# The expert stage of a decoder block: six experts written out, against hardware loops on four engines

## The chip, the core and the metric

The kernel runs on one core of a Trainium2 chip. A core has five engines with an instruction stream each: PE (TensorE, matrix products), DVE (VectorE), ACT (ScalarE), POOL (GpSimd) and SP (SyncE, which here only issues DMA transfers). Each stream is read by a sequencer of its own, and the streams wait for one another by semaphores. The time is the device time of one execution in microseconds (us); lower is better.

## What is computed

Two layers of a decoder on 256 tokens of 1024 channels, all in float32. Each layer has a mixer (a gated MLP over positions beside multi-head latent attention) and a channel part with SwiGLU: dense in the first layer, in the second eight experts of which each token takes two. The change is in the experts:

```python
logits = (xt @ w_router + b_router).astype(jnp.float32)
top_val, top_idx = lax.top_k(logits, TOP_K)          # 2 of 8
gates = jax.nn.softmax(top_val, axis=-1)
...
def run_block(args):                                  # one expert on up to 128 tokens
    tok, e = args
    xb = x_pad[tok]
    hb = jax.nn.silu(xb @ w1[e]) * (xb @ w3[e])       # 1024 -> 3584
    return hb @ w2[e]                                 # 3584 -> 1024
...
out = jnp.zeros((N + 1, D), h.dtype).at[buf_tok].add(yb)[:N]   # yb weighted by the gates
```

## The kernel before

Weights come from HBM in chunks of 128 x 2048 floats (1 MB). SP loads each into one of seven slots of `raw`. For full float32 accuracy a chunk is split in two parts that PE reads faster: ACT copies `raw` to `hi` (rounded, L511), DVE computes `lo = raw - hi` (L883), both into one of three slots, and PE makes three products per piece, `hi*hi`, `lo*hi` and `hi*lo` (`three`, L1358 to L1360; each matmul has its own weight load, which the profile calls PEld). One chunk is twelve such matmuls of 512 columns. At the end of a chunk PE raises the semaphore `used`, which frees the `hi`/`lo` slot for ACT; DVE raises `raw_done`, for which PE waits before it starts a chunk and SP before it loads into the `raw` slot again.

An expert is an item of 42 chunks (`PER_ITEM`), in seven groups `g`: two chunks of `w1`, two of `w3`, and two of `w2` of the group before. `w2` of the last group is done in the next item, so each item is entangled with its neighbour. `item(i, par, first, ahead)` writes out one item on an engine; `par` says which half of the token tiles it uses. Besides the chunks, an item holds work for the next one: `select` (DVE, at `g == 2`) copies the next expert's positions and gates and writes the matrices that pick its tokens (`one_hot`; and `gate_hot`, the same with the gate weights, into `r4[:, 256:512]`), `slot_rows` and `rows` find the rows to gather, `turn_rows`, `gathered` and `gathered_lo` bring the next tokens in (the last two groups).

Items 0 and 7 have other arguments than the six between. All eight are written out: on SP by `for i in range(1, EXPERTS)` (L342), on ACT, DVE and PE by `for i in range(1, EXPERTS - 1)` (L778, L1340, L1762). So item numbers are constants, and so are the values of all waits. POOL's eight steps are written out too. Behind them stands a hardware loop over up to three spare items for experts with more than 128 tokens (`If(spare > 0)`, L347, L784, L1345, L1767). With these inputs there is no spare item (the 336 loads of expert weights are 8 x 42), and each engine jumps over it. In this loop the same functions are called with `i` in a register, so the code for that exists. Each engine's order is the order of the code; there is no scheduler. `Fori` repeats a body on the one engine that calls it, with no barrier between engines.

Of the kernel before, what the change touches and what calls it, by code (L numbers as in the profile page):

```python
# [25 lines left out]
T = SEQ // P  # L26
# [15 lines left out]
EXPERTS = 8  # L42
# [133 lines left out]
def build(nc, A, out):  # L176
    with ExitStack() as ctx:
# [32 lines left out]
        ms, rstd = sb("mean_sq", [P, 4]), sb("rstd", [P, 4])  # L210
# [103 lines left out]
        @block.sync  # L314
        def _(sp):
            sp.dma_start(cols[:, :], A["cols"]).then_inc(consts_in, 16)
            sp.dma_start(cbc[:, :], A["c"].to_broadcast([P, D])).then_inc(cbc_in, 16)
            for r, (kind, n, q) in enumerate(STREAM):
                if r >= NRAW:
                    sp.wait_ge(raw_done, r - NRAW + 1)  # L320
                if kind == "ada":
                    l, v = ADA[n]
                    src, e = A["w_ada"][l, v, q], CH
                else:
                    _, t, (a, b), e = WEIGHTS[n]
                    src = A[t][a, b]
                sp.dma_start(raw[:, r % NRAW, 0:e], src).then_inc(raw_full[r % NRAW], 16)
                if r == 1:
                    sp.dma_start(x[:, :, :], A["x"].rearrange("b (t p) d -> p (b t) d", p=P)).then_inc(x_in, 16)

            def item_loads(i, chunks, expert):
                for c, kind, g, half, before_ in chunks:
                    sp.wait_ge(raw_done, i * PER_ITEM + (NR + c - NRAW + 1))
                    e = expert - 1 if before_ else expert
                    src = A["moe_" + kind]
                    src = src[e, g, half] if isinstance(e, int) else \
                        src[bass.ds(e, 1), g, half, :, :].rearrange("e p n -> p (e n)")
                    slot = (NR + c) % NRAW
                    sp.dma_start(raw[:, slot, :], src).then_inc(raw_full[slot], 16)

            item_loads(0, item_order(True), 0)
            for i in range(1, EXPERTS):  # L342
                item_loads(i, item_order(False), i)
            item_loads(EXPERTS - 1, LAST, EXPERTS - 1)
            sp.wait_ge(route_ready, 1)
            spare = sp.value_load(info[0:1, ITEMS:ITEMS + 1], min_val=0, max_val=SPARE)
            with sp.If(spare > 0):  # L347
                with sp.Fori(EXPERTS, ITEMS) as i:
                    with sp.If(i < spare + EXPERTS):
                        expert = sp.value_load(info[0:1, bass.ds(i, 1)], min_val=0, max_val=EXPERTS - 1)  # L350
                        item_loads(i, item_order(True) + LAST, expert)
            for t in range(T):
                sp.wait_ge(x_done, 2 * L * T - T + 1 + t)
                sp.dma_start(out[0, t * P:(t + 1) * P, :], x[:, t, :]).then_inc(out_done, 16)
            sp.wait_ge(out_done, 16 * T)
# [130 lines left out]
        def _(act):  # L486
# [252 lines left out]
            def item(i, par, first, ahead):  # L739
                if first:  # L740
                    for h in range(2):
                        gather_hi(i, par, h)
                    if not ahead:
                        item_hi(i, 0, 2)
                at = [(3 if ahead else 2) if first else 0]

                def upto_c(c):
                    item_hi(i, at[0], c + 1)
                    at[0] = max(at[0], c + 1)

                for g in range(NG):
                    c = spot("w1", g, 1, first)
                    if g == 1 and not first:
                        upto_c(c + 1)
                        weighted_y(i - 1, 1 - par, spot("w2", NG - 1))
                    upto_c(min(c + 2, PER_ITEM - 1))
                    act.wait_ge(used, i * PER_ITEM + (NW + c + 1))
                    act.activation(hs[g], ps[:, g % 2, :], ACT.Silu).then_inc(m_silu, 1)
                    if g:
                        hidden_hi(i, g - 1)  # L760
                    elif not first:
                        hidden_hi(i - 1, NG - 1)
                    if g == 3 and not ahead:
                        act.wait_ge(m_gt, i - (EXPERTS - 2))
                        act.activation(r4[:, 512:512 + SEQ], ps[:, 7, 0:SEQ], ACT.Copy).then_inc(m_gtc, 1)
                    if ahead and g >= NG - 2:
                        upto_c(min(c + 3, PER_ITEM - 1))
                        gather_hi(i + 1, 1 - par, g - (NG - 2))
                upto_c(PER_ITEM - 1)
# [5 lines left out]
                copy_y(i, PER_ITEM - 1)  # L775

            item(0, 0, True, True)
            for i in range(1, EXPERTS - 1):  # L778
                item(i, i % 2, False, True)
            item(EXPERTS - 1, 1, False, False)  # L780
            drain(EXPERTS - 1)
            act.wait_ge(route_ready, 1)
# [14 lines left out]
        def _(dve):  # L797
# [346 lines left out]
            for t in range(T):  # L1144
                dve.wait_ge(router_full, t + 1)
                m = dve.tensor_tensor(lg[:, t, :], ps[:, R_BANK[t], 0:E], rb[:, :], ALU.add)
            link(m)

            for t in range(T):
# [3 lines left out]
                m = dve.tensor_tensor(eq[:, t], other, own, ALU.is_equal)  # L1153
            link(m)
            for t in range(T):
                m = dve.tensor_tensor(eq[:, t], eq[:, t], lt_mask[:, :, :], ALU.mult)
# [51 lines left out]
            def one_hot(t, value):  # L1208
                return dve.tensor_scalar(r4[:, t * P:(t + 1) * P], slots[:, :], pg[:, t:t + 1], value, ALU.is_equal, ALU.mult)

            def gate_hot(t):
                return dve.tensor_scalar(r4[:, 256 + t * P:256 + (t + 1) * P], slots[:, :], pg[:, t:t + 1], vals[:, t, 2:3],
                                         ALU.is_equal, ALU.mult)

            def select(i, by_row):

                dve.tensor_copy(pg[:, :], pos_tab[:, :, bass.ds(i, 1)].rearrange("p t o -> p (t o)"))
                dve.tensor_copy(vals[:, :, 2], gate_tab[:, :, bass.ds(i, 1)].rearrange("p t o -> p (t o)")).then_inc(v_loop, 1)
                dve.wait_ge(v_loop, i + 1)
                for t in range(T):  # L1220
                    m = one_hot(t, 1.0 if by_row else rstd[:, T + t:T + t + 1])
                    if not by_row or i == EXPERTS - 1:
                        m = gate_hot(t)
                m.then_inc(m_pos, 1)

            def select_first():
# [110 lines left out]
                dve.memset(small[:, 0:1], 0.0)  # L1337

            item(0, 0, True, True)
            for i in range(1, EXPERTS - 1):  # L1340
                item(i, i % 2, False, True)
            item(EXPERTS - 1, 1, False, False)
            drain(EXPERTS - 1)
            spare = dve.value_load(info[0:1, ITEMS:ITEMS + 1], min_val=0, max_val=SPARE)
# [10 lines left out]
        def _(pe):  # L1355
# [403 lines left out]
                    scatter(i, q, DRAIN[q])  # L1759

            item(0, 0, True, True)
            for i in range(1, EXPERTS - 1):  # L1762
                item(i, i % 2, False, True)
            item(EXPERTS - 1, 1, False, False)
            drain(EXPERTS - 1)
            spare = pe.value_load(info[0:1, ITEMS:ITEMS + 1], min_val=0, max_val=SPARE)
# [78 lines left out]
```

## Time and profile before

| | us |
|---|---|
| median of 3 runs | 1586.76 |
| lowest and highest | 1585.12, 1586.84 |
| the profiled execution | 1586.84 |
| its span, first to last instruction | 1585.1 |
| TensorE clock granted, mean | 0.986 |

The page of the profile gives the busy time of each engine, the chain of work that ended last (92% of it PE, 5% DVE) and the costliest groups of instructions. The expert stage begins near 607 us and ends near 1568 us. Instructions of a sequencer alone (branches, waits, register operations; marked with a q behind the engine, as PEldq) are not counted as busy. A granted clock of 1.00 is 2.4 GHz and 0.50 is 1.2 GHz.

### The profile page before, as it was taken

The page shows a single profiled execution, that of the slowest core. Times are in us where ns is not written, and L with a number is a line of the kernel's source. Part 1 is how long each engine was busy: PE and PEld are TensorE (multiplying, and loading weights), DVE is VectorE, ACT ScalarE, POOL GpSimd, SP SyncE. Part 2 cuts the span into 40 slices and gives each one's busy share as a digit, 9 for nine tenths or more (in the row PEclk, how much of TensorE's full clock was granted, in tenths as well). Part 3 has the DMA queues.
Part 4 walks back from the last instruction along what each step waited for, and adds up shares of the span by engine and source line. Part 5 has one row for each costly group of instructions (what it writes and reads, how often), then busy time and mean ns, then how long its engine had stood idle before and what let it go on. Part 6 is the DMA issues. An engine that isn't in the chain of part 4 may idle for free.

```text
span 1585.1 us, 19800 instructions
## 1 busy us (share of the span) xinstructions
PE 1515.7 (96%) x8112; PEld 1310.0 (83%) x8112; DVE 1333.5 (84%) x1298; ACT 1011.8 (64%) x869; POOL 73.8 (5%) x103
## 2 busy tenths in 40 slices
PE   2999989999899988999999999999999999999996
PEld 2899979999789977888888888888888888888884
DVE  6688977775888768999999999999999998998885
ACT  3673444444466445777777777777777777777773
POOL 6000000000000000000000000000000000000000
PEclk9999999999999998999999999999999999999998
DMA  9757957986755855999999999999999999999990
GB/s 374 284 195 276 343 224 292 299 265 208 234 209 212 258 208 204 364 382 359 390 381 358 397 383 354 401 379 356 401 372 363 397 379 362 388 377 367 409 382 29
DMA packets 72977, 507.98 MB, mean 320 GB/s; under 512 B 8240, under 2 KB 8368, under 8 KB 14128
## 3 DMA queue, kind: packets, MB, share of 16 engines
q1 hardware_dynamic: 68672, 491.94, 81.9%
q0 software_dynamic: 4208, 14.70, 3.3%
q8 instruction: 66, 1.08, 0.3%
q14 instruction: 31, 0.25, 0.0%
HBM read 499.78 MB, written 6.83 MB: 320 GB/s over the span
## 4 chain that ended last, share of the span: by engine, by line
PE 92%; DVE 5%; ACT 1%; DMA 1%; issue 1%; SPq 0%; DVEq 0%; ACTq 0%
PE ps L1358 29%; PE ps L1360 28%; PE ps L1359 28%; PE ps L1728 2%; DVE raw L816 1%; PE ps L1375 1%; DMA x_tok<-in_x_dram 1%; PE ps L1496 1%; PE ps L1479 1%; DVE r L902 1%; DVE x_tok L940 1%; ACT r L523 0%; DVE lo L855 0%; PE ps L1425 0%; DVE hT_lo L908 0%
## 5 line engine op out<-in xcount | busy, mean ns | idle before, releaser
L883 DVE TENSOR_TENSOR lo<-raw,hi 128x2048 fp32r<-128x2048 f32 x336 | 766.3, 2290 | 94.5 <-ACT hi L511 93.7
L511 ACT ACTIVATE hi<-raw 128x2048 fp32r<-128x2048 f32 x336 | 644.6, 1919 | 198.3 <-PE ps L1360 198.3
L1358 PE MATMUL ps<-hi,hT_hi 128*128 128x512 f32 (+2 forms) x1088 | 427.6, 393 | 12.2 <-DVE hT_lo L908 8.8
L1360 PE MATMUL ps<-hi,hT_lo 128*128 128x512 f32 (+2 forms) x1088 | 421.0, 387 | 0.0
L1359 PE MATMUL ps<-lo,hT_hi 128*128 128x512 f32 (+2 forms) x1088 | 420.5, 386 | 0.0
L1358 PEld LDWEIGHTS ps<-hi,hT_hi 128*128 128x128 f32 x1088 | 205.3, 189 | 58.0 <-issue 13.1
L855 DVE TENSOR_TENSOR lo<-raw,hi 128x2048 fp32r<-128x2048 f32 (+2 forms) x87 | 189.9, 2187 | 62.7 <-ACT hi L495 61.3
L1360 PEld LDWEIGHTS ps<-hi,hT_lo 128*128 128x128 f32 x1088 | 205.2, 189 | 41.0
L1359 PEld LDWEIGHTS ps<-lo,hT_hi 128*128 128x128 f32 x1088 | 205.5, 189 | 37.6
L1358 PE MATMUL ps<-hi,bT_hi 128*128 128x512 f32 (+1 forms) x576 | 224.6, 390 | 1.8 <-DVE bT_lo L1272 1.8
L1359 PE MATMUL ps<-lo,bT_hi 128*128 128x512 f32 (+1 forms) x576 | 223.7, 388 | 0.0
L1360 PE MATMUL ps<-hi,bT_lo 128*128 128x512 f32 (+1 forms) x576 | 223.5, 388 | 0.0
L495 ACT ACTIVATE hi<-raw 128x2048 fp32r<-128x2048 f32 (+2 forms) x87 | 158.4, 1824 | 93.1 <-PE ps L1360 89.7
L1358 PE MATMUL ps<-hT_hi,hi 128*128 128x256 f32 x608 | 173.0, 285 | 1.7 <-DVE hT_lo L908 1.7
L1360 PE MATMUL ps<-hT_hi,lo 128*128 128x256 f32 x608 | 172.1, 283 | 0.0
L1359 PE MATMUL ps<-hT_lo,hi 128*128 128x256 f32 x608 | 172.0, 283 | 0.0
L1358 PEld LDWEIGHTS ps<-hi,bT_hi 128*128 128x128 f32 x576 | 108.6, 188 | 26.0 <-issue 2.8
L1360 PEld LDWEIGHTS ps<-hi,bT_lo 128*128 128x128 f32 x576 | 108.5, 188 | 21.8
L1359 PEld LDWEIGHTS ps<-lo,bT_hi 128*128 128x128 f32 x576 | 108.4, 188 | 20.9
L816 DVE SCALAR_TENSOR_TENSOR raw<-raw,c_rows 128x1024 f32<-128x1024 f32 x96 | 113.6, 1221 | 9.9 <-DMA raw<-in_w_ada_dram 9.8
L1358 PEld LDWEIGHTS ps<-hT_hi,hi 128*128 128x128 f32 x608 | 116.7, 192 | 2.6 <-DVE hT_lo L908 1.4
L1359 PEld LDWEIGHTS ps<-hT_lo,hi 128*128 128x128 f32 x608 | 116.6, 192 | 0.3
(255 smaller groups left out, 1177.9 us busy)
## 6 DMA issues: line engine op xcount, KB each, us to landing
raw<-in_moe_w_dram SPq DMA_DIRECT2D x336, 1024.0 KB, 7.1
raw<-in_w_ada_dram SPq DMA_DIRECT2D x48, 1024.0 KB, 6.1
raw<-in_w_fg_dram SPq DMA_DIRECT2D x11, 1024.0 KB, 7.4
raw<-in_w_fu_dram SPq DMA_DIRECT2D x11, 1024.0 KB, 6.7
raw<-in_w_fd_dram SPq DMA_DIRECT2D x11, 1024.0 KB, 6.9
raw<-in_w_ga_dram SPq DMA_DIRECT2D x8, 1024.0 KB, 5.9
raw<-in_w_gb_dram SPq DMA_DIRECT2D x8, 1024.0 KB, 5.2
raw<-in_w_ab_dram SPq DMA_DIRECT2D x8, 1024.0 KB, 4.9
```

The lines of the kernel that those rows point to most:

```text
L495: act.activation(hi[:, s % NSPLIT, 0:e], raw[:, r % NRAW, 0:e], ACT.Copy).then_inc(hi_done, 1)
L511: act.activation(hi[:, s, :], raw[:, slot, :], ACT.Copy).then_inc(hi_done, 1)
L816: m = dve.scalar_tensor_tensor(w, w, 1.0, cbc[:, :], ALU.mult, ALU.mult, accum_out=av[:, k:k + 1])
L855: dve.tensor_tensor(lo[:, s % NSPLIT, 0:e], raw[:, r % NRAW, 0:e], hi[:, s % NSPLIT, 0:e].bitcast(f32), ALU.subtract).then_inc(raw_done, 1)
L883: dve.tensor_tensor(lo[:, s, :], raw[:, slot, :], hi[:, s, :].bitcast(f32), ALU.subtract).then_inc(raw_done, 1)
L902: m = dve.tensor_scalar(hf[:, k, :], ps[:, X_BANKS[n][b], (k % 2) * SEQ:(k % 2 + 1) * SEQ], AB[:, n, 0, k:k + 1], AB[:, n, 1, k:k + 1], AL ...
L940: dve.scalar_tensor_tensor(x[:, t, :], y_sb[:, t, :], rstd[:, t:t + 1], x[:, t, :], ALU.mult, ALU.add).then_inc(x_done, 1)
L1358: pe.matmul(o, wh, mh, start=first, stop=False)
L1359: pe.matmul(o, wh, ml, start=False, stop=False)
L1360: return pe.matmul(o, wl, mh, start=False, stop=last)
L1375: m = pe.matmul(ps[:, X_BANKS[n][k // 2], (k % 2) * SEQ + t * P:(k % 2) * SEQ + (t + 1) * P], x[:, t, k * P:(k + 1) * P], diag[:, t, :], s ...
L1728: m = pe.transpose(ps[:, 6, c * P:(c + 1) * P], hs[g][:, c * P:(c + 1) * P], ident[:, :])
```

## The change

SP's seven items become one hardware loop of seven passes. On ACT, DVE and PE the six items become a loop of three passes with two items in the body, one for each value of `par`. `i` is then a register (or computed from one), and so are the values of the waits in the body. On DVE `select` no longer depends on whether `i` is the last item: it writes `gate_hot` every time. In the changed kernel the lines of DVE and PE have numbers one higher, since ACT's part is a line longer.

```diff
             item_loads(0, item_order(True), 0)
-            for i in range(1, EXPERTS):
+            with sp.Fori(1, EXPERTS) as i:
                 item_loads(i, item_order(False), i)
             item_loads(EXPERTS - 1, LAST, EXPERTS - 1)
...
             item(0, 0, True, True)
-            for i in range(1, EXPERTS - 1):
-                item(i, i % 2, False, True)
+            with act.Fori(0, EXPERTS // 2 - 1) as j:
+                item(j * 2 + 1, 1, False, True)
+                item(j * 2 + 2, 0, False, True)
             item(EXPERTS - 1, 1, False, False)
...
                 for t in range(T):
-                    m = one_hot(t, 1.0 if by_row else rstd[:, T + t:T + t + 1])
-                    if not by_row or i == EXPERTS - 1:
-                        m = gate_hot(t)
+                    one_hot(t, 1.0 if by_row else rstd[:, T + t:T + t + 1])
+                    m = gate_hot(t)
                 m.then_inc(m_pos, 1)
```

The six lines of ACT stand in the same words for DVE and PE.

What moves in the streams. PE, from the last matmuls of an even item to the next item, before:

```order
L1358 MATMUL ps<-hi,bT_hi 128x512
L1359 MATMUL ps<-lo,bT_hi 128x512
L1360 MATMUL ps<-hi,bT_lo 128x512
L1358 MATMUL ps<-hi,hT_hi 128x512 [waits raw_done,m_x,m_silu]
L1359 MATMUL ps<-lo,hT_hi 128x512
L1360 MATMUL ps<-hi,hT_lo 128x512
```

and in the changed kernel the end of the loop's body:

```order
L1359 MATMUL ps<-hi,bT_hi 128x512
L1360 MATMUL ps<-lo,bT_hi 128x512
L1361 MATMUL ps<-hi,bT_lo 128x512
L1763 REGISTER_ALU
L1763 COMPARE_AND_BRANCH
```

and the head of the body, to which the branch goes back:

```order
L1763 ISA
L1672 ISA [waits m_silu]
L1666 ISA [waits m_x]
L1359 MATMUL ps<-hi,hT_hi 128x512 [waits raw_done]
L1360 MATMUL ps<-lo,hT_hi 128x512
```

Two rows are added at the loop's end and three at its head, and two of the three waits now stand on register instructions (ISA and REGISTER_ALU). The body is 1197 rows on PE (1084 of them matmuls), 265 on DVE, 240 on ACT and 102 on SP.

DVE at `select`, in an item between the first and the last, before:

```order
L1272 TENSOR_TENSOR bT_lo<-ps,bT_hi 128x4x128 [waits m_hh]
L883 TENSOR_TENSOR lo<-raw,hi 128x2048 [waits hi_done] x2
L1268 TENSOR_TENSOR r<-r,ps 128x512 [waits used,m_silu]
L883 TENSOR_TENSOR lo<-raw,hi 128x2048 [waits hi_done] x4
L1272 TENSOR_TENSOR bT_lo<-ps,bT_hi 128x4x128 [waits m_hh]
L1217 COPY pg<-pos_tab 128x2
L1218 COPY slot_vals<-gate_tab 128x2
L1209 TENSOR_SCALAR r<-slots,pg 128x128 [waits v_loop]
L1209 TENSOR_SCALAR r<-slots,pg 128x128
L883 TENSOR_TENSOR lo<-raw,hi 128x2048 [waits hi_done] x2
```

and in the changed kernel:

```order
L1272 TENSOR_TENSOR bT_lo<-ps,bT_hi 128x4x128 [waits m_hh]
L1218 ISA
L1218 COPY pg<-pos_tab 128x2
L1219 REGISTER_ALU
L1219 COPY slot_vals<-gate_tab 128x2
L1220 REGISTER_ALU
L1210 TENSOR_SCALAR r<-slots,pg 128x128 [waits v_loop]
L1213 TENSOR_SCALAR r<-slots,pg,slot_vals 128x128
L1210 TENSOR_SCALAR r<-slots,pg 128x128
L1213 TENSOR_SCALAR r<-slots,pg,slot_vals 128x128
L883 REGISTER_ALU
L884 TENSOR_TENSOR lo<-raw,hi 128x2048 [waits hi_done]
```

Two `gate_hot` (L1213) and register instructions ahead of each wait are added. ACT, the head of its loop in the changed kernel, from the branch into it:

```order
L778 UNCONDITIONAL_BRANCH
L778 ISA
L510 ISA [waits raw_full2]
L511 ACTIVATE hi<-raw 128x2048 [waits used]
L510 REGISTER_ALU [waits raw_full3]
L511 ACTIVATE hi<-raw 128x2048 [waits used]
L757 REGISTER_ALU
L758 ACTIVATE r<-ps 128x512 [waits used]
```

The same stretch was only the ACTIVATE rows before; each of the others carries the register value, or the first of two waits, of the one behind it.

## Rows read from the trace of the kernel before

**Rows 1.** busy time by engine, page part 1: busy us (share) xinstructions

```profile
PE 1515.7 (96%) x8112; PEld 1310.0 (83%) x8112; DVE 1333.5 (84%) x1298; ACT 1011.8 (64%) x869; POOL 73.8 (5%) x103
```

**Rows 2.** busy by stretch, experts 1 to 6: us busy (x) per engine, PEclk, DMA

```profile
722.87:1442.74 719.87, 719.39 (x3275) 592.98 (x3276) 653.20 (x448) 538.01 (x355) 28.91 (x12) 1.00 0.99 378
```

**Rows 3.** waits in that stretch: who waited for whom, us, times, longest

```profile
PEld ps L1358 <- issue: 3.5, 8, 0.5
PEld ps L1358 <- DVE lo L883: 2.4, 6, 0.4
```

**Rows 4.** timeline, weight loads at chunk starts: start us, us, what, [idle before]

```profile
961.94 0.19 PEld L1358 LDWEIGHTS ps<-hi,hT_hi 128*128 128x128 f32 x1 [0.47 <-issue]
...
1006.82 0.19 PEld L1358 LDWEIGHTS ps<-hi,bT_hi 128*128 128x128 f32 x1
...
1009.54 0.19 PEld L1358 LDWEIGHTS ps<-hi,bT_hi 128*128 128x128 f32 x1
...
1197.83 0.19 PEld L1358 LDWEIGHTS ps<-hi,bT_hi 128*128 128x128 f32 x1
...
1200.97 0.19 PEld L1358 LDWEIGHTS ps<-hi,hT_hi 128*128 128x128 f32 x1 [0.47 <-issue]
...
1206.90 0.19 PEld L1358 LDWEIGHTS ps<-hi,hT_hi 128*128 128x128 f32 x1
...
1320.50 0.19 PEld L1358 LDWEIGHTS ps<-hi,hT_hi 128*128 128x128 f32 x1 [0.47 <-issue]
...
1440.10 0.19 PEld L1358 LDWEIGHTS ps<-hi,hT_hi 128*128 128x128 f32 x1 [0.47 <-issue]
```

**Rows 5.** timeline of DVE and ACT around the start of expert 5

```profile
1195.16 2.29 DVE L883 TENSOR_TENSOR lo<-raw,hi 128x2048 fp32r<-128x2048 f32 x1 [0.31 <-ACT hi L511]
...
1198.57 6.70 DVE L883 TENSOR_TENSOR lo<-raw,hi 128x2048 fp32r<-128x2048 f32 x3
...
1198.31 1.92 ACT L511 ACTIVATE hi<-raw 128x2048 fp32r<-128x2048 f32 x1 [0.80 <-PE ps L1360]
1201.03 1.92 ACT L511 ACTIVATE hi<-raw 128x2048 fp32r<-128x2048 f32 x1 [0.80 <-PE ps L1360]
```

**Rows 6.** single lines of the sequencers: duration ns min/median/max, first and last start

```profile
L1767 PEldq COMPARE_BRANCH  x1: 3854/3854/3854, 1569.9 to 1569.9; - x1
...
L1766 PEldq FUSED_REGOPS  x1: 165/165/165, 1569.6 to 1569.6; - x1
...
L1345 DVEq COMPARE_BRANCH  x1: 76/76/76, 1574.4 to 1574.4; - x1
...
L784 ACTq COMPARE_BRANCH  x1: 45/45/45, 1568.7 to 1568.7; - x1
```

**Rows 7.** the program's end: PE's timeline, stretch 1569 to 1575, its DMA queue

```profile
1569.04 3.70 PE L1749 MATMUL ps<-r 128*128 128x512 f32 x8 [1.17 <-ACT r L730]
...
1569.00:1575.00 6.00, 3.70 (x8) 1.44 (x8) 2.81 (x5) 1.49 (x2) 0.00 (x0) 1.00 0.04 8
...
q8 instruction: 2, 0.03, 2.7%
```

**Rows 8.** PE's semaphore instruction ahead of a chunk, expert 5

```profile
L1665 PEldq EVENT_SEMAPHORE  x1: 51/51/51, 1200.9 to 1200.9; - x1
```

**Rows 9.** DMA issues, page part 6: xcount, KB each, us to landing

```profile
raw<-in_moe_w_dram SPq DMA_DIRECT2D x336, 1024.0 KB, 7.1
```

**Rows 10.** timeline of DVE behind `select`, experts 3 and 6

```profile
1004.26 4.57 DVE L883 TENSOR_TENSOR lo<-raw,hi 128x2048 fp32r<-128x2048 f32 x2
...
1363.17 4.48 DVE L883 TENSOR_TENSOR lo<-raw,hi 128x2048 fp32r<-128x2048 f32 x2
```

**Rows 11.** busy by stretch where PE stood idle, columns as in rows 2

```profile
612.70:617.60 4.90, 3.34 (x15) 2.77 (x16) 4.69 (x11) 3.14 (x4) 0.00 (x0) 1.00 0.59 221
...
1558.70:1560.60 1.90, 0.07 (x1) 0.08 (x1) 1.77 (x2) 0.60 (x1) 0.00 (x0) 1.00 0.00 0
...
1560.80:1564.10 3.30, 3.30 (x9) 2.52 (x9) 0.00 (x0) 0.00 (x0) 0.00 (x0) 0.50 0.00 0
```

More of the change, by code:

```diff
@@ L1339, in _ @@
             item(0, 0, True, True)
-            for i in range(1, EXPERTS - 1):
-                item(i, i % 2, False, True)
+            with dve.Fori(0, EXPERTS // 2 - 1) as j:
+                item(j * 2 + 1, 1, False, True)
+                item(j * 2 + 2, 0, False, True)
             item(EXPERTS - 1, 1, False, False)
@@ L1761, in _ @@
             item(0, 0, True, True)
-            for i in range(1, EXPERTS - 1):
-                item(i, i % 2, False, True)
+            with pe.Fori(0, EXPERTS // 2 - 1) as j:
+                item(j * 2 + 1, 1, False, True)
+                item(j * 2 + 2, 0, False, True)
             item(EXPERTS - 1, 1, False, False)
```

## Prediction

> **What bounds the kernel now.** I read the busy table first: TensorE (PE) is busy 96% of the span, VectorE (DVE) 84%, ScalarE (ACT) 64% [rows 1]. The table by stretch comes second. From 722.87 to 1442.74 us, six experts long, PE is busy 719.39 of 719.87 us at the full granted clock, DVE 653, and the DMA share is 0.99 [rows 2]. So whatever is added there hurts only if it delays PE. The waits of that stretch come third: in 720 us PE's weight loads wait 2.4 us for the `lo` copy and 3.5 us for "issue" [rows 3]. Work goes round in a ring: PE frees a slot, ACT makes `hi` (1.92 us), DVE makes `lo` (2.29 us) [rows 5], PE uses the pair three chunks later.
>
> The timeline says how tight the ring is. At the start of the sixth expert (i = 5) the last chunk of the one before starts on PE at 1197.83, and its `lo` ended at 1195.16 + 2.29 = 1197.45, 0.38 us sooner. The next chunk starts at 1200.97, 3.14 us later instead of the 2.72 us between the chunk starts at 1006.82 and 1009.54, because DVE comes late there: three `lo` back to back from 1198.57 [rows 4, 5]. An expert takes 1320.50 - 1200.97 = 119.53 us.
>
> **The loops.** Experts 1 to 6 become a loop of three passes over two experts on PE, DVE and ACT; SP's loop has seven passes of one. Each of the first three engines therefore takes a backward branch twice, SP six times. Three things are new: the branch, register instructions ahead of waits, and `gate_hot` in every `select`.
>
> *The branch.* The trace of before holds one taken branch per engine, the jump over the spare experts. On DVE and ACT it took 76 and 45 ns, on PE 3854 ns, and around PE's the queue q8 read two blocks of instructions [rows 6, 7]. PE's jump skips 609 rows of the order with 554 matmuls, the other two 138 and 121. The new backward jump of PE crosses 1197 rows, further still, so I charge it as a fetch: 3.854 us. I read the Trainium skill, "Runtime: NRT & Kernel Launch", section "Instruction fetch mechanics", the same way: a taken branch whose target lies outside the two pages held must wait for the page. The trace agrees for PE. Another rule speaks for a much lower price and is rival C.
>
> What of 3.854 us does PE feel? Matmuls are handed over in advance: at 1569.04 eight matmuls of L1749 start which last 3.70 us, and the branch behind them began at 1569.9, beneath them [rows 6, 7]. So the branch starts when the last chunk has been handed over, at about 1197.5 (its `lo` end), plus one register instruction, taken as the 51 ns of PE's semaphore instruction [rows 8]: 1197.55. It ends at 1201.40. Three "ISA" rows stand at the head of the body; as a fused register operation costs 165 ns [rows 6], 0.50 us, plus 0.07 us from semaphore to weight load: 1201.97. Without a branch that load came at 1200.97. Loss: 1.0 us per branch when the DMA queues are idle as they were at 1569 to 1575 (DMA share 0.04) [rows 7]. In the expert stage the share is 0.99 [rows 2], and a 1 MB load lands after 7.1 us [rows 9] while one is wanted every 2.72: about 2.6 are under way at a time, and behind one of them the fetch would be 2.7 us later. I take 0.6, nearer to no delay because instructions have a queue of their own. So 1.6 us per branch, bounds 1.0 and 3.7, and 3.2 us for two.
>
> *DVE's and ACT's branches* cross 265 and 240 rows, about twice what they jumped cheaply, so they may cost 0.05 to 3.9 us. ACT's pass ends with the `hi` of 1198.31, DVE's with the second of the three `lo` from 1198.57; the `hi` of 1201.03 and the third `lo` (about 1203.0) are the first work of the next pass [rows 5]. At 3.9 us ACT's branch would end at 1198.4 + 3.9 = 1202.3, two fused operations of 165 ns [rows 6] bring its `hi` to 1202.6, it is done at 1204.6, and `lo` at 1206.9; DVE's own branch (from 1200.3) ends sooner than that. PE needs this chunk at 1206.90 [rows 4] plus its own 1.6 us = 1208.5. Hidden, by 1.6 us. If PE's branch were free the margin would be zero, and these branches would cost 0 to 0.5 us. SP's loads run seven slots ahead: the slot ring is 7 x 2.72 = 19 us, of which landing takes 7.1 and `hi` and `lo` 4.3; 7 us are left against 3.9. Nothing.
>
> *Register instructions.* One stands before nearly every wait. On PE it runs while the sequencer would wait anyway (a chunk is handed over within a chunk's 2.72 us). On DVE and ACT it runs below a working instruction of 0.6 to 2.3 us. Exposed is only the chain of `rows()`, four short instructions that follow one another by semaphores with `lo` behind them. Of its register rows one is a fused operation (165 ns on PE, rows 6), most of it beside a copy; I charge 0.06 us per expert, bounds 0 and 0.3. Over six: 0.4 us. SP has one load to issue per 2.72 us and several us of lead: nothing.
>
> *gate_hot.* Before, only `select(7)` did it, so the trace has both forms. In expert 3 the `lo` behind it starts at 1004.26, 42.32 us after PE's start at 961.94; in expert 6, with `gate_hot`, at 1363.17, 42.67 us after 1320.50 [rows 4, 10]. So `lo` is 0.35 us later, and a margin takes most of it: expert 6 lasts 1440.10 - 1320.50 = 119.60 us, 0.07 more than expert 5 [rows 4]. Six times: 0.4 us, bounds 0.4 and 1.4.
>
> **Sum.** 3.2 + 0.4 + 0.4 = 4.0 us on the profiled execution's own 1586.84 us (span 1585.1 and 1.7 around it), which is 0.08 above the median of 1586.76: 1590.8 us. About 0.2%, 3.2 us, is what a measurement of this kernel tells from no change, so the forecast is just on the slower side.
>
> **Rivals.**
>
> A, the forecast: 1.0 to 2.0 us per back edge, 1589.6 to 1592. Chance 0.42.
>
> B, each back edge costs more. The fetch takes the whole 2.7 us more, and PE's idle time brings the half clock. The trace shows it once near the end: from 1558.7 to 1560.6 PE was busy 0.07 of 1.90 us, and from 1560.8 to 1564.1 the granted clock was 0.50, with 9 matmuls in 3.30 us [rows 11]; that is 1.2 instead of 2.4 GHz and costs half the stretch, 1.6 us. Per edge 1.0 + 2.7 + 1.6 = 5.3, twice 10.6, plus 0.8: 1598.2. For it: total idle at the edge would be 0.4 + 3.7 us. Against: the stretch from 612.7 holds 1.5 us in which PE was idle and stays at 1.00 [rows 11], and at the forecast's 1.6 us the idle time, 2.0 us, lies near either example. Chance 0.24.
>
> C, the back edge is nearly free, as DVE's and ACT's in the trace: then only 0.8 us is added: 1587.6, no measurable change. The 3854 ns would be something else of that one place (it is PE's last instruction, with matmuls still running). The Trainium skill, "Advanced Engine Details and Errata", section "Control Flow Timing", gives about 108 ns for a compare-and-branch; by that the two edges would cost 0.2 us. The trace has 45 and 76 ns and the one 3854. Chance 0.19.
>
> D, faster. At present an instruction with two waits is preceded by a separate semaphore instruction, 51 ns on PE [rows 8]; in the loop the first wait rides on the register instruction instead, ahead of the last one. Where DVE is late, PE's gap would shrink, at the expert's start above all (3.14 - 2.72 = 0.42 us). In six experts PE's loads wait 3.5 + 2.4 = 5.9 us [rows 3]; all of it gone, with the 0.8 us still to pay, gives 1581.7. It decides only if the edge is free and more than 0.5 us per expert comes back, while what it can remove directly is under 0.1 us at each place. Chance 0.08.
>
> E, the register instructions are not hidden: PE, DVE and ACT each pay at every chunk. With 252 chunks in the loop and 0.05 us each, 12.6 us more: 1600 or above. Against it: the margin of 0.38 us and more before each chunk. Chance 0.07.
>
> Slower by over 0.2% is above 1589.9: three quarters of A, B and E, 0.63. Same: the rest of A and C, 0.29. Faster 0.08. The range leaves out D, most of E and the far end of B: 1587.2 to 1598.5.
>
> **What would show it.** PE's compare-and-branch twice with about 4 us, and an idle PE of 1 to 2 us beyond the present 0.4 at the starts of experts 3 and 5, nothing such at 2, 4 and 6. DVE and ACT branches long or short, without PE waiting for `lo` behind them. Expert 4 or 6 lasting about 119.6 to 119.7 us (119.53 before) checks the small terms; 120 or more would be E. Branches of 0.1 us on PE would refute the largest step; granted clock 0.5 in the expert stage would be B.

## The result

The changed kernel takes 1602.63 us (median of 4 runs, 1599.17 to 1603.6) against 1586.75 us in the same comparison; the ratio is 1.0099, with a 95% interval of 1.0082 to 1.0116. The forecast was 1590.8 us, with a range of 1587.2 to 1598.5. The direction was right, the size was not: +15.9 us instead of +4.0.

The page of the changed kernel, parts 1 and 3 (columns as in rows 1; a queue's packets, MB, share):

```profile
PE 1519.5 (95%) x8112; PEld 1312.9 (82%) x8112; DVE 1334.7 (83%) x1310; ACT 1012.0 (63%) x869; POOL 73.7 (5%) x103
...
q8 instruction: 71, 1.16, 0.3%
q14 instruction: 25, 0.20, 0.0%
```

PE has the same 8112 matmuls, busy 3.8 us longer, in a span that is 15.6 us longer (1600.7 against 1585.1): most of the loss is idle time. q8, which brings PE's instructions, made 71 reads of 16 KB; before it made 66. One such read is called a block below; it holds 256 instructions, which the counts of the experiments bear out. (The 1197 rows of PE's loop are, with one weight load for each matmul and the sequencer's own, 2290 instructions in the trace, nearly nine blocks.) The waits of PE's weight loads over the six experts, beside [rows 3]:

```profile
PEld ps L1361 <- issue: 8.7, 2, 5.0
PEld ps L1359 <- DVE lo L884: 6.5, 11, 3.1
PEld ps L1359 <- issue: 2.1, 2, 1.7
```

The line to notice is the first. L1361 is the third matmul of a group of three; no semaphore is waited for there, and [rows 3] has no such entry. Now it waits twice, 8.7 us in all, for nothing that a semaphore shows. Busy time by stretch shows where (columns as in rows 2):

```profile
720.00:955.00 235.00, 235.00 (x1073) 193.93 (x1072) 213.75 (x152) 175.63 (x118) 9.70 (x4) 1.00 0.99 379
955.00:975.00 20.00, 13.99 (x53) 10.79 (x52) 11.45 (x7) 8.76 (x5) 0.00 (x0) 0.83 0.82 320
975.00:1195.00 220.00, 220.00 (x1003) 181.58 (x1002) 199.29 (x139) 164.37 (x109) 9.61 (x4) 1.00 0.96 370
1195.00:1222.00 27.00, 21.18 (x90) 16.87 (x89) 17.86 (x15) 14.92 (x10) 0.00 (x0) 0.87 0.88 330
1222.00:1450.00 228.00, 228.00 (x1043) 188.36 (x1042) 206.98 (x147) 171.10 (x114) 9.62 (x4) 1.00 0.97 372
```

Outside the two short stretches PE is busy without a break. Both short ones hold a back edge of PE's loop. The timeline of the weight loads at the first (the counterpart of 961.94 in rows 4):

```profile
961.87 0.19 PEld L1361 LDWEIGHTS ps<-hi,bT_lo 128*128 128x128 f32 x1
965.14 0.19 PEld L1359 LDWEIGHTS ps<-hi,hT_hi 128*128 128x128 f32 x1 [3.08 <-DVE lo L884]
965.25 0.19 PEld L1360 LDWEIGHTS ps<-lo,hT_hi 128*128 128x128 f32 x1
969.22 0.29 PEld L1361 LDWEIGHTS ps<-hi,hT_lo 128*128 128x128 f32 x1 [3.79 <-issue]
969.39 0.34 PEld L1359 LDWEIGHTS ps<-hi,hT_hi 128*128 128x128 f32 x1
969.82 0.33 PEld L1360 LDWEIGHTS ps<-lo,hT_hi 128*128 128x128 f32 x1
```

There are three losses, one behind the other. PE stands until 965.14, for its branch; that the row names DVE's `lo` only means that this semaphore came last by the profile, for the sequencer was inside the branch from 959.2 for 5.6 us (below). It then does two matmuls and stands again until 969.22. From there the loads are 0.43 us apart instead of 0.227: half the clock, 1.2 instead of 2.4 GHz. The same happens at 1210.74 and 1216.00. The branch lines, q8 in the stretches 958 to 970 and 1204 to 1217, and the clock after each second gap:

```profile
L1763 PEldq COMPARE_BRANCH  x3: 83/4191/5626, 959.2 to 1452.4; - x3
...
q8 instruction: 2, 0.03, 1.1%
...
q8 instruction: 2, 0.03, 0.9%
...
969.10:972.60 3.50, 3.38 (x8) 2.70 (x9) 0.00 (x0) 0.00 (x0) 0.00 (x0) 0.50 0.97 396
1215.90:1219.40 3.50, 3.40 (x9) 2.73 (x10) 0.00 (x0) 0.00 (x0) 0.00 (x0) 0.57 0.89 346
```

Two blocks are read at each edge where the argument had one. When they are read shows in shorter stretches, 962 to 963 and 966.5 to 967.5:

```profile
q8 instruction: 1, 0.02, 6.7%
...
q8 instruction: 1, 0.02, 6.0%
```

The first read starts at 962.33, while the branch runs (959.15 to 964.78). The second starts at 966.99, 2.2 us after the branch has ended, and PE goes on 2.2 us behind that. The branch lines of the other engines' loops (ACT, DVE, SP):

```profile
L778 ACTq COMPARE_BRANCH  x3: 40/45/45, 959.9 to 1453.1; - x3
...
L1340 DVEq COMPARE_BRANCH  x3: 50/56/76, 961.8 to 1455.0; - x3
...
L342 SPq COMPARE_BRANCH  x7: 40/45/50, 820.1 to 1551.4; - x7
```

All are short. q14 brings the other engines' instructions, 8 KB at a time: its 31 reads become 25 with their loops and stay 31 where PE alone has one (the first experiment). Between 930 and 1560 us, while these three engines go round their loops, it reads nothing at all.

The account in the profiled executions goes by the start of each expert on PE (its first weight load): 723.77, 843.08, 965.14, 1089.94, 1210.74, 1336.27 and 1455.67 us in the changed kernel, so experts 1 to 6 last 119.31, 122.06, 124.80, 120.80, 125.53 and 119.40 us. Against the mean of the two undisturbed ones, 119.355, the first stalls cost 2.7 and 1.4 us (they fall into experts 2 and 4), the second stalls with the half clock 5.4 and 6.2 (experts 3 and 5). Unrounded that is 15.8 us. Beside it 0.9 us were lost ahead of expert 1 (723.77 against 722.87), and 1.1 us was won over the six experts, which took 119.50 to 119.60 each before.

### The profile page after: what moved, and what is told of

The parts are those of the page before. It is cut to its first block, busy times and chain, and to the rows that moved or that the text cites. A ratio compares the mean times of both kernels' runs of the same rounds, so it can differ in the third digit from the quotient of the medians.

```text
span 1600.7 us, 21289 instructions
## 1 busy us (share of the span) xinstructions
PE 1519.5 (95%) x8112; PEld 1312.9 (82%) x8112; DVE 1334.7 (83%) x1310; ACT 1012.0 (63%) x869; POOL 73.7 (5%) x103
## 4 chain that ended last, share of the span: by engine, by line
PE 91%; DVE 5%; ACT 1%; issue 1%; DMA 1%; SPq 0%; DVEq 0%; ACTq 0%
PE ps L1359 29%; PE ps L1361 28%; PE ps L1360 28%; PE ps L1729 2%; DVE raw L817 1%; PE ps L1376 1%; DMA x_tok<-in_x_dram 1%; PE ps L1497 1%; PE ps L1480 1%; DVE r L903 1%; DVE x_tok L941 1%; DVE lo L884 1%; ACT r L523 0%; DVE lo L856 0%; PE ps L1426 0%
## 5 line engine op out<-in xcount | busy, mean ns | idle before, releaser
L884 DVE TENSOR_TENSOR lo<-raw,hi 128x2048 fp32r<-128x2048 f32 x336 | 764.7, 2290 | 108.2 <-ACT hi L511 107.5
L1361 PE MATMUL ps<-hi,hT_lo 128*128 128x512 f32 (+2 forms) x1088 | 422.4, 388 | 7.9 <-issue 7.9
L1361 PEld LDWEIGHTS ps<-hi,hT_lo 128*128 128x128 f32 x1088 | 206.0, 189 | 50.1 <-issue 8.7
L1361 PE MATMUL ps<-hi,bT_lo 128*128 128x512 f32 (+1 forms) x576 | 223.6, 388 | 0.0
L1361 PE MATMUL ps<-hT_hi,lo 128*128 128x256 f32 x608 | 172.1, 283 | 0.0
L1361 PEld LDWEIGHTS ps<-hi,bT_lo 128*128 128x128 f32 x576 | 108.4, 188 | 21.9
```

What stands on the lines that cost most here:

```text
L884: dve.tensor_tensor(lo[:, s, :], raw[:, slot, :], hi[:, s, :].bitcast(f32), ALU.subtract).then_inc(raw_done, 1)
L1361: return pe.matmul(o, wl, mh, start=False, stop=last)
```

## The experiments

The kernels were timed in three groups, each with the kernel before on the same chip (its medians: 1585.87, 1585.89 and 1585.28 us); ratios are to that. An "edge" is PE's backward branch; its cost is read as the surplus of the expert before it (first stall) and behind it (second stall and half clock). "The head" is the loop's first instruction.

### Whose loop is it?

**Only PE's loop, in the kernel before.**

```
 item(0, 0, True, True)                      # in PE's part alone
-for i in range(1, EXPERTS - 1): item(i, i % 2, False, True)
+with pe.Fori(0, EXPERTS // 2 - 1) as j:
+    item(j * 2 + 1, 1, False, True)
+    item(j * 2 + 2, 0, False, True)
```

> Only PE's loop of the change, in the kernel before; SP, ACT and DVE are unrolled as before and gate_hot stays in select(7) alone. Theory 1 (the whole loss is PE's two back edges: a serial fetch of the loop's first block, a second stall two matmuls later when the next block is fetched, and the half clock after it): two gaps of 8 to 10 us in all at the starts of experts 3 and 5, about +7.5 us each, so +15 to +16 us, 1602 us, like the changed kernel. Theory 2 (the loops of the four engines together, for example DVE's and ACT's register instructions or their fetches colliding with PE's at the edge, make the loss): +4 to +8 us, 1591 to 1595.

Measured: 1601.12 us, ratio 1.0098 (1.0082 to 1.0113). PE's loop alone makes the whole loss. First stalls 3.1 and 2.2 us, second ones with the half clock 6.6 and 6.6.

**Everything but PE's loop**: the changed kernel with PE's part unrolled again.

> The changed kernel with PE unrolled as before; SP, ACT and DVE still loop and gate_hot is in every select. Theory 1 (PE's edges are all): no gap at experts 3 and 5, experts of 119.3 to 119.6 us, -1 to +1 us against the kernel before, 1586 to 1588. Theory 2 (the other loops share in the loss): +7 us or more, 1594 or above.

Measured: 1584.86 us, ratio 0.9996 (0.9987 to 1.0005). Experts last 119.45 to 119.52 us. Its waits in the six experts, as in [rows 3]:

```profile
PEld ps L1359 <- issue: 3.9, 13, 0.4
PEld ps L1359 <- DVE lo L884: 2.0, 6, 0.3
```

The total, 5.9 us, is the kernel before's to a tenth: with loops on SP, ACT and DVE and `gate_hot` everywhere, PE waits as little as before. Together the two kernels put the loss into PE's part, not yet into its cause.

### Where the head lies

Each kernel is the changed one with one argument more, which lays the loop's first instruction at a given slot of a block (and adds a jump into the loop); only the slot differs:

```
-with pe.Fori(0, EXPERTS // 2 - 1) as j:
+with nc.Fori(0, EXPERTS // 2 - 1, engines=[pe.engine], head_slot={pe.engine: 0}) as j:
```

**Head at the start of a block.**

> The changed kernel with the head of PE's loop laid at the start of a fetch block instead of wherever the code before it ends. Theory 1 (the second stall comes from the head lying 7 to 9 instructions before a block's end): the first stall of 3 to 4 us stays, the second one goes; if the half clock goes with it +3 us per edge, 1593; if it stays +4.5 us per edge, 1595.5. Theory 2 (the second stall and the half clock belong to any backward branch, wherever its head lies): nothing changes, 1602.

Measured: 1588.5 us, ratio 1.0021 (1.0010 to 1.0032). The second stall is gone from both edges, and with it the half clock: the stretch behind the first edge is all matmuls at full clock. What is left is a first stall of 1.5 and 1.4 us. Theory 1's mechanism holds; its total, 1593, was 4.5 us too high, since it kept a first stall of 3 to 4 us.

```profile
962.84 0.19 PEld L1359 LDWEIGHTS ps<-hi,hT_hi 128*128 128x128 f32 x1 [1.89 <-issue]
...
1203.00 0.19 PEld L1359 LDWEIGHTS ps<-hi,hT_hi 128*128 128x128 f32 x1 [1.74 <-issue]
...
L1763 PEldq COMPARE_BRANCH  x2: 4216/4329/4442, 958.0 to 1198.4; - x2
...
963.00:967.00 4.00, 4.00 (x18) 3.30 (x19) 2.65 (x2) 1.41 (x2) 0.00 (x0) 1.00 0.92 350
```

The branches still take 4.4 and 4.2 us. This kernel is the one that the forecast describes (1590.8 us, 1.6 us per edge). q8's second read is still made: it starts 3.2 and 3.7 us after the two branches have ended, with most of the first block still to run, so it isn't put off until the engine comes to the block's end. The eleven runs spread from 1585.32 to 1594.79 us (the kernel before, 1584.36 to 1587.23); what the slow ones among them did, no trace shows.

**Head 17 instructions before a block's end.**

> The changed kernel with the head of PE's loop at slot 239 of a block of 256, so 17 instructions before its end (in the changed kernel 7 of them ran before the second stall). Theory 1 (two fetches in series; the second is asked for when the first has landed and takes 4.4 to 5.6 us, while PE uses an instruction every 0.113 us): 17 instructions cover 1.9 us instead of 0.8, so the second gap shrinks from 3.35 and 4.5 us to 2.2 and 3.4 us, and the edges cost about 6.5 us each: 1599 to 1600. Theory 2 (the place of the head in the block does not matter, the start of a block is special in another way): as the changed kernel, 1602.

Measured: 1598.78 us, ratio 1.0081 (1.0066 to 1.0097).

```profile
961.47 0.19 PEld L1359 LDWEIGHTS ps<-hi,hT_hi 128*128 128x128 f32 x1 [2.06 <-issue]
...
962.72 0.19 PEld L1359 LDWEIGHTS ps<-hi,hT_hi 128*128 128x128 f32 x1
966.37 0.28 PEld L1360 LDWEIGHTS ps<-lo,hT_hi 128*128 128x128 f32 x1 [3.46 <-issue]
...
966.30:971.50 5.20, 5.13 (x12) 4.06 (x13) 0.65 (x1) 1.91 (x1) 0.00 (x0) 0.50 0.74 293
```

Count what PE did between the stalls. From 961.47 to 962.72 there are 7 loads and 7 matmuls, 14 instructions, and ahead of them the three register instructions at the head of the body: 17, exactly what was left of the block. In the changed kernel it is 3 + 2 loads + 2 matmuls = 7. So the second stall does stand at the block's end, at both edges. The second gaps on PE are 3.0 and 2.9 us (3.35 and 4.5 in the changed kernel); the total fits Theory 1, though the first gap shrank less than it said and the second more.

**Head 48 instructions before the end.**

> The same with the head at slot 208, 48 instructions before the block's end. Theory 1: 48 instructions cover 5.4 us, the second fetch is hidden at one edge at least, no half clock: 1588 to 1590, like the head at slot 0. Theory 2: 1602.

Measured: 1590.98 us, ratio 1.0034 (1.0025 to 1.0043), a little above Theory 1's range. No second stall at the first edge and a short one, 0.40 us, at the second. The first edge still had the half clock, which Theory 1 had ruled out, after a first stall of 2.5 us; the second, after 1.75 us, had not:

```profile
963.37 0.19 PEld L1359 LDWEIGHTS ps<-hi,hT_hi 128*128 128x128 f32 x1 [2.53 <-DVE lo L884]
...
963.40:966.40 3.00, 3.00 (x8) 2.40 (x9) 2.13 (x1) 0.00 (x0) 0.00 (x0) 0.60 0.97 339
...
1205.04 0.19 PEld L1359 LDWEIGHTS ps<-hi,hT_hi 128*128 128x128 f32 x1 [1.75 <-issue]
...
1205.00:1209.00 4.00, 3.96 (x17) 3.30 (x18) 2.99 (x2) 1.57 (x2) 0.00 (x0) 1.00 0.90 324
...
1210.30 0.19 PEld L1360 LDWEIGHTS ps<-lo,hT_hi 128*128 128x128 f32 x1 [0.40 <-issue]
```

The 0.40 us stand where a block's end has to be: from the branch to that gap there are 22 loads, 21 matmuls and 5 register instructions, 48 in all. The block behind came 5.6 us after the branch's end here, and 48 instructions did not quite last so long.

7, 17, 48 and 256 instructions left give 1602.63, 1598.78, 1590.98 and 1588.5 us: a loss that falls as the rest of the block grows, until the rest covers the next read. That the stall moved behind the 7th, 17th and 48th instruction is the stronger evidence, since the totals also hold first stalls of changing length.

### The fetch asked for ahead

**A prefetch hint on the back edge** (an instruction at the head of the body tells the engine's fetch of the branch to come):

```
+with nc.Fori(0, EXPERTS // 2 - 1, engines=[pe.engine], hint_back_edge=True) as j:
```

> The changed kernel with a prefetch hint on PE's back edge (the engine is told of the branch ahead of it), nothing else. Theory 1 (the loss is a fetch that is only asked for when the branch runs): the first stall goes, the block of the loop's head is held when PE branches; the second block may still be fetched late, since the head lies near a block's end, so +0 to +4 us per edge, 1587 to 1595. Theory 2 (the stall is the engine's own restart at a branch, not the fetch): no change, 1602.

Measured: 1588.27 us, ratio 1.0013 (1.0004 to 1.0022).

```profile
L1763 PEldq BRANCH_PREFETCH_HINT  x3: 36/36/55, 720.0 to 1197.3; - x3
...
L1763 PEldq COMPARE_BRANCH  x3: 88/364/388, 958.2 to 1435.6; - x3
...
1439.93 0.19 PEld L1361 LDWEIGHTS ps<-hi,hT_lo 128*128 128x128 f32 x1
1443.06 0.29 PEld L1359 LDWEIGHTS ps<-hi,hT_hi 128*128 128x128 f32 x1 [2.94 <-issue]
...
1443.00:1446.50 3.50, 3.44 (x9) 2.72 (x10) 0.24 (x1) 0.42 (x1) 0.00 (x0) 0.53 0.99 367
```

The same branches take 0.36 and 0.39 us instead of 4 to 6, and the experts around both edges last 119.35 to 119.37 us: free. The price has moved to the exit, 4.3 us in all. In the last pass the hint is wrong, the branch falls through, and behind six more matmuls, the sixth with its load at 1439.93, PE's loads stand 2.94 us and PE runs at half clock after that. The block after the exit had not been fetched.

The place of the stall also tells where this loop's head lies. Behind the exit 13 instructions run before it, and the body has 2291, which is nine blocks less 13: so the head is no longer 7 instructions before a block's end, as in the changed kernel, but at a block's start. This kernel is therefore to be compared with the one at slot 0 (1588.5 us). Against that one the hint removed the first stalls, at the price of the exit; the second stalls were gone already, by the place of the head.

**The hint with the exit moved away from a block's end**, by putting the head at slot 96:

> The changed kernel with the prefetch hint on PE's back edge and the loop's head at slot 96, so that the loop's exit lies some 175 instructions before its block's end instead of 14. The hint made both back edges free and cost 4.2 us at the exit, where the wrong block had been fetched. Theory 1 (the block behind the exit is asked for when the branch is resolved, so that 175 instructions cover it): the exit's stall goes, experts of 119.3 us throughout, 1584 to 1585, 1 to 2 us below the kernel before. Theory 2 (it is asked for only when the engine runs over the block's end): the stall of 3 us and the half clock stay, only later in the seventh expert: 1588.

Measured: 1584.14 us, ratio 0.9992 (0.9983 to 1.0001). Expert 7's start waits 0.40 us and there is no stall behind it; PE's waits over six experts (second row: the stretch itself) are down to 4.1 us from the 5.9 of [rows 3]:

```profile
PEld ps L1359 <- DVE lo L884: 4.1, 12, 0.4
...
722.36:1438.44 716.08, 716.08 (x3265) 590.91 (x3264) 651.20 (x457) 536.42 (x354) 28.92 (x12) 1.00 0.98 379
```

The head has 160 instructions of its block left here, which covers the second read. This is the fastest kernel of the study: clearly faster than the changed one, and not to be told from the kernel before.

**The hint with the head 17 instructions before the end.**

> The changed kernel with the prefetch hint and the loop's head at slot 239, 17 instructions before its block's end. Theory 1 (the hint fetches the head's block alone; the block behind it is asked for when the engine is there): the first gap goes, a second one of 2 to 3 us stays at each edge, with the half clock after it 3 to 5 us per edge: 1591 to 1594. Theory 2 (once the hint is given, the block behind the head comes with it, or the edge has time enough to fetch both): free edges, 1584 to 1585.

Measured: 1592.09 us, ratio 1.0045 (1.0030 to 1.0061). The total is Theory 1's. The profiled execution was the quickest of the four (1586.97; the others 1591.9 to 1594.2) and shows one second gap of 0.95 us at 963.64, again at the block's end (four register instructions now, the hint among them, seven loads and six matmuls: 17), and none at the other edge. So the hint brings the head's block alone and is no cure for a head near a block's end. Where the slower three spent 5 to 7 us more, no trace shows; that it was the same gap, longer, is likely and not shown.

```profile
963.64 0.19 PEld L1360 LDWEIGHTS ps<-lo,hT_hi 128*128 128x128 f32 x1 [0.95 <-issue]
...
1443.38 0.19 PEld L1361 LDWEIGHTS ps<-hi,hT_lo 128*128 128x128 f32 x1 [0.64 <-issue]
```

The second row is the exit: the gap comes behind 30 instructions, 17 more than in the kernel with the hint alone, as the places of the two heads have it. q8's read for it starts at 1441.06, 0.8 us before the sequencer passes a semaphore (1441.82) that still lies ahead of the block's end. So it was asked for before the engine came there, as the kernel at slot 96 says too. From the branch (resolved at 1436.5) to the block's arrival it is 6.9 us.

### The small terms

**`gate_hot` in every select, the kernel before otherwise.**

```
-    m = one_hot(t, ...)
-    if not by_row or i == EXPERTS - 1:
-        m = gate_hot(t)
+    one_hot(t, ...)
+    m = gate_hot(t)
```

> The kernel before with gate_hot in every select, everything unrolled: the small term of the prediction alone. By the prediction +0.07 us per expert, +0.4 us in all, no measurable change: 1586.3; by its upper bound +1.4 us. What a rival would say (gate_hot is what keeps the changed kernel's experts from being shorter still): 0.3 us or more per expert, +2 us.

Measured: 1587.81 us, ratio 1.0019 (1.0010 to 1.0028), as much as the rival said. But the experts last 119.60 to 119.70 us, 0.1 more than before, which is 0.6 us in all. The rest is at the end of the program, in DVE's gap behind its jump over the spare experts (kernel before, then this one):

```profile
1575.05 0.06 DVE L1350 MEMSET small<- 128x1 f32 x1 [1.46 <-issue]
```

```profile
1575.98 0.06 DVE L1349 MEMSET small<- 128x1 f32 x1 [3.81 <-issue]
```

The branch took 76 ns in both; the first instruction behind it came 2.35 us later. (0.6 and 2.35 are 2.95 us; the interval of the ratio is 1.6 to 4.4. The two profiled executions differ by 0.9 alone, as expert 1 starts 2.0 us sooner in this one.) `gate_hot` adds 12 instructions to DVE's stream, and that raised a suspicion that the next two kernels test.

**12 instructions of another kind instead of `gate_hot`**, placed where DVE waits for PE anyway:

```
 def drain(i):
     hidden_lo(i, NG - 1)
+    if isinstance(i, int):
+        for k in range(12):
+            dve.memset(padt[:, k:k + 1], 0.0)
```

> The kernel before with 12 tiny memsets (59 ns each) added on DVE near the end, inside the 9.8 us in which it waits for PE, and nothing else. gate_hot in every select had added just 12 instructions to DVE's stream, and behind DVE's jump over the spare experts the gap had grown from 1.46 to 3.81 us, 2.35 of that kernel's +1.9 us. Theory 1 (those 12 instructions had moved a fetch block's end to just behind the jump's target): the gap is 3.8 us here too, +2.35 us, 1588.2. Theory 2 (gate_hot itself had cost the 2 us): gap 1.46 us, 1586.

Measured: 1588.44 us, ratio 1.0018 (1.0009 to 1.0028).

```profile
1576.74 0.06 DVE L1354 MEMSET small<- 128x1 f32 x1 [3.92 <-issue]
```

The same gap, from twelve memsets of 59 ns that ran while DVE was idle. And a read of q14 lies inside the long gap of both kernels, from 1574.04 in that with `gate_hot` and from 1574.67 here (q14 in 1572.9 to 1576.7 us):

```profile
q14 instruction: 1, 0.01, 0.9%
```

In the short gap of the kernel before, 1573.6 to 1575.05, there is none. Where the stream's blocks end is worth 0.2% here by itself.

**`gate_hot` with 46 more memsets**, so that the block's end lies elsewhere:

> The kernel with gate_hot in every select and 46 tiny memsets more on DVE near the end, which move the block's end on by 46 instructions. Theory 1 (place of the block's end): the gap behind the jump is 1.5 us again and only gate_hot's own cost is left, 0.1 us per expert, +0.6 us: 1586.5. Theory 2 (gate_hot itself): 1587.8 or more.

Measured: 1586.92 us, ratio 1.0008 (0.9998 to 1.0017).

```profile
1573.44 0.06 DVE L1353 MEMSET small<- 128x1 f32 x1 [1.48 <-issue]
```

The gap is short again, with no read of q14 in it, the experts last 119.63 us, and what `gate_hot` costs by itself is that 0.1 us per expert.

### A candidate for the fastest

```
-with act.Fori(0, EXPERTS // 2 - 1) as j:        # the same on DVE; on PE with hint and slot 96
+with act.Fori(0, EXPERTS // 2 - 2) as j:
     item(j * 2 + 1, 1, False, True)
     item(j * 2 + 2, 0, False, True)
+item(EXPERTS - 3, 1, False, True)
+item(EXPERTS - 2, 0, False, True)
```

> A candidate for the fastest: hint and head at slot 96 on PE; on PE, DVE and ACT the loop covers experts 1 to 4 (two passes), experts 5 and 6 are unrolled, and gate_hot stands only in the last select, as in the kernel before. Theory 1 (edges free, register instructions carry waits and save 0.15 us per looped expert, gate_hot costs 0.1 per expert): 0.3 to 0.6 us below the kernel with hint and slot 96, 1583.7. Theory 2 (the place of block ends in the new layout decides instead): 1586 or more, with a gap of 2 to 4 us somewhere at the exit or in the tail.

Measured: 1586.09 us, ratio 1.0001 (0.9992 to 1.0010): the miss is Theory 1's. Theory 2 named the total, but its gap of 2 to 4 us is nowhere in the trace. The looped experts last 119.33 to 119.43 us, the unrolled fifth and sixth 119.84 and 119.62, so unrolling two gave back 0.8 us and leaving out `gate_hot` did not make up for it. (0.3 of it is the fifth, which is that much longer than an unrolled expert of the kernel before; no run says why.) Another 1.6 us of the 2.2 between the two profiled executions is the half clock near the program's end, which the last section comes to.

## Why the forecast fell short, step by step

**One fetch per edge.** This is the step that failed: "I charge it as a fetch: 3.854 us", one, and PE's surplus worked out from its end. The jump does need a fetch, and its price was near: the ten back edges without a hint took 4.2 to 6.3 us and cost PE 1.4 to 3.3 us in the first stall, 2.1 on average, against my 1.6. The overlap was right as well: at all ten edges PE felt the branch less 2.8 to 2.9 us, and my working had 3.854 less 2.85. (In it, the three register instructions count 0.50 us, and they took 0.3.) What is missing is what comes behind it, which I had at nothing: a second stop of PE of 3.35 and 4.5 us at the two edges, with the half clock 11.6 of the 15.6 us. A jump leaves PE with the one block that it asked for. The next is asked for when the first has come: its read starts 2.2 to 3.7 us after the branch has ended, at all ten edges. It is there 4.4 to 6.0 us after the branch's end (964.78 to 969.22 is the shortest), at the eight edges where PE had to wait for it. The rest of the first block has to last that long; at 0.113 us per instruction (a load and a matmul every 0.227 us) it takes some 40 to 55 instructions, and the head happened to lie 7 before the end. Slots 0 and 96 (this with the hint) show no second stall, slot 208 one of 0.40 us, 239 and the changed kernel long ones. The evidence had been in [rows 7]: q8 read two blocks around PE's one jump. I quoted it and priced one.

The Trainium skill, "Runtime: NRT & Kernel Launch", section "Instruction fetch mechanics", says that prefetch is purely sequential over two held blocks and that a jump outside them waits for the target's block. The trace agrees: the branches whose target was not held took 4.2 to 6.3 us, those whose target was held 0.31 to 0.39. By that rule the second wait follows too, since after such a jump the block behind the target is not held either. I did not draw that conclusion.

**The half clock.** Rival B had it, as one of two surcharges on an edge: 1.6 us. Measured, 7 and 5 matmuls wholly at 0.43 instead of 0.227 us and two partly, 1.9 and 1.4 us at the two edges. B's other surcharge, 2.7 us for a first fetch that waits behind loads, came in part: the two branches took 1.8 and 0.3 us more than 3.854. Most of the time went into a second fetch, and so B's total of 1598.2 falls short too. I gave B 0.24 because the forecast's idle time of 2.0 us lay between my two examples. With about 6 us of idle time at each edge the question doesn't arise.

**DVE's, ACT's and SP's branches.** 40 to 76 ns, at the cheap end of 0.05 to 3.9 us. q14, which reads 8 KB at a time, made 25 reads instead of 31, and none between 930 and 1560 us: these bodies stay with their engines. Nothing was paid, as said, though not because it was hidden.

**Register instructions.** Forecast +0.4, measured a small gain: with loops on SP, ACT and DVE an expert lasts 119.48 us against 119.63 unrolled with the same `gate_hot`, and with PE's loop on top (hint, slot 96) 119.35. PE's wait at an expert's start falls with them, from 0.47 to 0.41 and 0.35 us, which fits rival D's mechanism; no run takes it by itself. D overrated it, 0.3 us per expert instead of up to 1.0. Rival E's total, 1600 or above, holds the measured time, and its mechanism is refuted: undisturbed experts got shorter, 119.31 against 119.53 us. A total can be met for a wrong reason.

**`gate_hot`.** Forecast 0.07 us per expert, measured 0.1. The term is right within its bounds. Its side effect on the place of a block's end, 2.35 us, was not thought of, and the changed kernel does not have it: its gap is 1.46 us, its DVE stream being laid out differently by the loops.

**The sum.** Forecast 3.2 + 0.4 + 0.4 = 4.0 us. In the trace 4.15 (two first stalls) + 11.6 (two second stalls with half clock) - 1.1 (the experts) + 0.9 ahead of expert 1 = 15.6 us, all of it. The term that had no place in the forecast is the 11.6. The 0.9 us were lost before any back edge, and no experiment was made for them; in the other kernels' traces expert 1 starts anywhere from 720.91 to 722.87 us, so they may be no effect at all. By the median, the kernel with only the first stalls, 1588.5 us, is what this forecast was a forecast of.

## To carry to other kernels

PE's backward jump, over a body larger than what PE holds, cost two waits for a fetch and not one where the head lay near the end of a block: look at how many instructions run after such a jump before the engine stops again, and move the head. The hint takes away the first wait alone, and the exit has then to be looked at too. Whether instructions come in time depends on their place in the stream, so an edit can cost 2 us in a part of the program that it doesn't touch; before an edit's own work is blamed, add the same number of idle instructions to the old kernel and time that. And a wait that has "issue" as its cause, at a line that never waits, is read together with the queue that brings the instructions.

## What the runs showed that was not expected

- PE's branch takes 4.2 to 6.3 us at the edges, while loads fill the queues (DMA share 0.9 and above), and PE's last jump, with idle queues, 3.3 to 3.9 us in every kernel. My bound of 2.7 us for waiting behind loads was nearly reached once.
- PE's jump into a block that was read before takes 0.31 to 0.39 us (the hinted edges, and the entry into the loops with a slot); DVE's, ACT's and SP's take 40 to 76 ns. A wrong hint has its price at the next block's end: PE's loads stood 2.94 us, with the half clock behind, when the end came 13 instructions behind the exit, and 0.64 us when it came 30 behind. With some 175 instructions in between it cost nothing.
- In the expert stage, PE gaps of 1.3 to 1.7 us were followed by the full clock; those of 2.1 us and more ended in the half clock, at once or behind the second gap, for 1.4 to 3.0 us more. One gap of PE, 1.84 us near the program's end, is the same in all 14 kernels and was followed by the half clock in 9 of them, the kernel before among them [rows 11], and by the full clock in 5. From expert 7's start to its last chunk the former take 124.6 us and the latter 123.1, where nothing else disturbs them. So 1.6 of the 3 us by which runs of one kernel differ can come from this place alone, and two profiles must be compared there before a difference of 0.1% is explained.
